# A three-block transformer kernel: recurrence scaling and gating order, row tails, attention buffers and decay weights rearranged

## Chip, cores, metric

The kernel runs on 1 core of one Trainium2 chip. The metric is the device time of one execution in microseconds (us); lower is better.

## What is computed

One input of 512 tokens x 1024 features, in float32, passes through three blocks. Each block is a mixer, a layer norm, a routed mixture of experts (MoE) and another layer norm. Cut to what matters here:

```python
# block 1: SSD (a chunked state-space scan, computed in this kernel as masked, decayed products) and
#          forgetting attention side by side, then w_out
y = y_diag + y_off + xs * d_skip                       # decay factors exp(a_cum_t - a_cum_s), causal
y = (y * silu(z)) * rsqrt(mean(square(y * silu(z))) + eps) * ssd_norm_g
probs = softmax(q k^T / 8 + F[t] - F[s])               # 8 heads of 64, causal
# block 2: differential attention, 8 heads, two softmaxes each
attn = p[:, :, 0] - lam * p[:, :, 1];  o = attn @ v;  o = o * rsqrt(mean(o*o) + eps) * subln_g * 0.8
# block 3: RWKV-7 time mix: token-shift mixes, low-rank w, a, g, and a recurrence per head
state = state * w_t + (state a_t) b_t + v_t k_t;  y_t = state r_t
y = groupnorm(y) * lnx_g + lnx_b + sum(r * k * r_k) * v;  out = (y * g) @ w_o
# each block: top-2 of 16, 32 and 32 experts (hidden size 512) per token, SwiGLU
```

## The kernel before

The program is a row of stages, each a block of five instruction streams (TensorE = PE, ScalarE = ACT, VectorE = DVE, GpSimd = POOL, SyncE = SP) that meet only at the stage's end. Within a stage the order on each engine is written out by hand and held together by semaphores; no scheduler reorders anything, so an instruction that waits holds all that stands behind it on its engine. Tokens lie in four tiles of 128 rows (j = 0 to 3). Weights of 2 MB a chunk go through a ring of six slots, which SP fills as the matmuls that used a slot finish; each expert has three such chunks. The stages, in order of time:

- `in_proj_stage` (block 1's projections), `ssd_and_attention_stage`, `project_and_experts(0)`.
- `norm_qkv_stage` (second norm of block 1, projections of block 2), `attention_stage`, `project_and_experts(1)`.
- `norm_rkv_stage` (second norm of block 2, projections of block 3), `wkv_stage` (the recurrence), `wkv_out_stage`, `project_and_experts(2)`, `last_norm_stage`.

**Decay weights** (L423 to L441, L738 to L858). For each of 8 heads a 128 x 1280 triangle of weights exp(min(0, decay)) is made. ACT writes the three off-diagonal pieces by Exp (`fade_off_diagonal`, L433). DVE writes the four diagonal 128 x 128 pieces as min(0, decay) (`clamp_diagonal`, L440). ACT takes Exp of these 512 columns (L781). DVE multiplies all 1280 columns with cb (L847), and PE multiplies per pair of heads (L744). Heads 0 to 2 are prepared in the stage before. Heads share four buffers, so heads 4 to 7 wait at L778 and L815 until the pair that used their buffer is through PE. Then `take_y` (L821, L822) adds the skip and gates, ACT squares (L763), PE sums (`sums`, L694, L695), and ACT turns the sums into inverse roots by Ln (L788) and Exp (L791), all ahead of its attention loop.

**Forgetting attention** (same stage, 16 steps) has three pairs of probability buffers. Each step: PE scores (L707, L710), DVE maxima (L827 to L829), ACT exponentials (L770), PE turns, ACT copies (L802), PE products, DVE copies out (L855). `norm_group` (L839) stands at steps 2 and 3 on DVE.

**Differential attention** (`attention_stage`, 32 steps) has the same loop with two pairs of buffers `prob`. In step s, PE does scores(s) (L922, L924), turn(s-2) (L938) and product(s-3) (L956). DVE does maxima(s) (L1020, L1021) and divide(s-1) (L1028, L1031, L1032), which combines the two softmaxes in place. turn(n) waits for divide(n).

**Row tails** (`norm_qkv_stage`, `norm_rkv_stage`). POOL gathers the experts' rows (L230). DVE adds them and takes statistics tile by tile (L244 to L252), ACT normalizes (L258, L260), PE turns the tile (`turn_rows`, L273), ACT takes it (`take_rows`, L281), and PE projects (L1601; L1772 for v). Before that PE runs 17 matmuls on constants (`keep_busy`, L265), of 128 x 512 in float32; each has two records in the trace. In `norm_rkv_stage` SP first loads eleven parameters on one semaphore. PE waits for the first nine, transposes `param_rows` (L1747), and only then turns rows; ACT waits for that transpose (L1786) before it normalizes tile 0. DVE mixes each tile with the tokens before (L1722 to L1712) for PE's v products.

**Recurrence** (`wkv_stage`). Eight turns, one for each pair of heads. In a turn PE doubles a triangular inverse in four rounds, each with two halves: squares (L2074), products (L2082), additions on DVE (`add_products`, L2346, which counts `d_tt` up by 8 a turn). The solves follow (`four`, L2090), each half copied out (L2272 by ACT, L2387 by DVE), then a serial chain of states (L2171, L2413). Between the first solves DVE prepares the next turn's operands (L2316, L2317). POOL finishes the rows of turn i-2:

```python
def finish_rows(n):
    pool.wait_ge(E["y_rstd"], n + 1)
    pool.wait_ge(d_tt, (n + 3) * 2 * ROUNDS)
    scaled_rows(pool, link, n, y_vars[n % 2])
    link(pool.tensor_tensor(rT[:, n, :], rT[:, n, :], y_added, ALU.add))
```

With n = i-2 this waits for all four rounds of turn i. The three operations are L1845, L1846, L1977, each over 128 x 512.

**After the recurrence** (`wkv_out_stage`). PE makes gate matmuls for eight column blocks (L1832, L1834; those of blocks 0 to 2, `EARLY_GATES`, come in the stage before) and transposes rows (L2493). ACT copies (L2504). DVE finishes the last pair's rows (L2509 to L2519) and only then multiplies gates in (L2523), block by block. PE's block c >= 4 waits for the multiplication of block c-4, whose PSUM bank it uses again.

## Time and profile before

| | us |
|---|---|
| time, median of 3 runs | 2727.61 (2724.8 to 2733.51) |
| profiled execution, its own time | 2733.16 |
| its span in the trace | 2731.4 |
| PE busy in it | 2366.0 (87%) |
| DVE, ACT, POOL busy | 1011.0, 564.9, 195.1 |
| granted TensorE clock, mean | 0.949 of full |

The profile is one execution, which took 5.6 us more than the median; its span leaves 1.8 us of its time outside. Times in its rows count from the start of the span. "Idle before" names who released a waiting engine. PEclk is the granted clock of TensorE in a stretch: 1.00 is 2.4 GHz, 0.50 is 1.2 GHz, and what lies between is a mixture of the two over the stretch.

### The profile page before, as it was taken

How to read it: one execution, taken by the hardware profiler on the slowest of the kernel's cores; microseconds unless marked ns; L12 is line 12 of the kernel's file. 1: busy time of each engine (PE TensorE's matmuls, PEld its weight loads, DVE VectorE, ACT ScalarE, POOL GpSimd, SP SyncE). 2: the span in 40 equal slices, each digit the busy share in tenths (PEclk: the TensorE clock that was granted, in tenths of full speed). 3: DMA queues.
4: the chain of work that ended last, by engine and by line, in shares of the span. 5: the costliest groups of instructions: out<-in, count | busy, mean ns of one | idle time of the engine just before them, and what ended most of it. 6: DMA issues, size and time to landing. Idle time of an engine off the chain costs nothing. (4 is left out here: it accounts for less than half of the span.)

```text
span 2731.4 us, 88107 instructions
## 1 busy us (share of the span) xinstructions
PE 2366.0 (87%) x38584; PEld 1611.1 (59%) x38585; DVE 1011.0 (37%) x2710; ACT 564.9 (21%) x1211; POOL 195.1 (7%) x309
## 2 busy tenths in 40 slices
PE   8997999999999888999767789978888988788982
PEld 4445557777444655777545533458777456566761
DVE  1216353333400854333212254046765353232324
ACT  2134211111300631111000031034332111011111
POOL 1002200000100010000000010012332100000001
PEclk9998999999999999999989889989999899899996
DMA  8211158976421006969999932000001269999995
GB/s 343 111 56 62 48 205 345 408 313 270 160 93 62 32 18 242 410 273 427 429 430 427 402 141 100 0 24 3 3 5 47 97 264 428 427 429 427 414 428 222
DMA packets 83423, 616.42 MB, mean 226 GB/s; under 512 B 19909, under 2 KB 40649, under 8 KB 49242
## 3 DMA queue, kind: packets, MB, share of 16 engines
q1 hardware_dynamic: 45664, 574.98, 50.9%
q10 hardware_dynamic: 31402, 20.06, 2.4%
q0 software_dynamic: 6224, 19.43, 2.2%
q8 instruction: 105, 1.72, 0.3%
q14 instruction: 28, 0.23, 0.0%
HBM read 582.92 MB, written 31.49 MB: 225 GB/s over the span
## 5 line engine op out<-in xcount | busy, mean ns | idle before, releaser
L1281 PE MATMUL ps<-ring,arena 128*32 128x128 f32 x13184 | 408.4, 283 | 104.7 <-DMA ring<-in_experts 71.9
L1281 PEld LDWEIGHTS ps<-ring,arena 128*32 128x32 f32 x13184 | 379.3, 114 | 146.3 <-DMA ring<-in_experts 69.8
L1258 PE MATMUL ps<-x_tok,arena 128*32 128x256 f32 x4768 | 291.3, 383 | 11.7 <-DVE arena L1396 8.3
L1489 DVE TENSOR_TENSOR arena<-arena,ps 128x64 f32<-128x64 f32 x292 | 64.8, 222 | 613.9 <-ACT arena L1341 613.9
L1341 ACT ACTIVATE arena<-ps 128x64 f32<-128x64 f32 x292 | 65.2, 223 | 1082.6 <-PE ps L1281 1082.6
L1281 PE MATMUL ps<-arena 128*32 128x128 f32 x5504 | 175.0, 287 | 45.5 <-DMA arena<-in_experts 37.0
L1258 PEld LDWEIGHTS ps<-x_tok,arena 128*32 128x32 f32 x4768 | 159.9, 111 | 89.4 <-issue 18.4
L1291 PE MATMUL ps<-ring,arena 128*32 128x256 f32 x3296 | 198.8, 380 | 12.4 <-DMA ring<-in_experts 12.2
L1281 PEld LDWEIGHTS ps<-arena 128*32 128x32 f32 x5504 | 160.8, 115 | 64.9 <-DMA arena<-in_experts 43.0
L1231 PE MATMUL ps<-ring,arena 128*128 128x512 f32 x384 | 172.3, 605 | 3.4 <-PEq L2460 1.7
L1291 PEld LDWEIGHTS ps<-ring,arena 128*32 128x32 f32 x3296 | 110.6, 110 | 83.6 <-DMA ring<-in_experts 20.3
L542 PE MATMUL ps<-xt_mem,ring 128*128 128x512 f32 x320 | 137.9, 593 | 0.0
L1231 PEld LDWEIGHTS ps<-ring,arena 128*128 128x128 f32 x384 | 73.1, 194 | 90.0 <-issue 89.7
L1476 DVE STREAM_TRANSPOSE arena<-ps 128x256 f32<-128x256 f32 x149 | 67.1, 450 | 148.7 <-PE ps L1258 148.7
L1775 PE MATMUL ps<-arena,ring 128*128 128x512 f32 x256 | 110.1, 593 | 0.0
L1601 PE MATMUL ps<-xt_mem,ring 128*128 128x512 f32 x256 | 110.0, 592 | 0.0
L542 PEld LDWEIGHTS ps<-xt_mem,ring 128*128 128x128 f32 x320 | 60.7, 190 | 76.4 <-issue 76.3
L1333 ACT ACT_TABLE_LOAD x73 | 93.7, 1283 | 33.0 <-DVE arena L1467 26.4
L1500 DVE COPY arena<-ps 128x256 f32<-128x256 f32 x146 | 62.0, 425 | 93.0 <-PE ps L1291 93.0
L1291 PE MATMUL ps<-xt_mem,arena 128*32 128x256 f32 x1376 | 83.4, 380 | 5.0 <-DMA xt_mem<-in_experts 3.9
L1775 PEld LDWEIGHTS ps<-arena,ring 128*128 128x128 f32 x256 | 48.6, 190 | 61.5 <-issue 61.5
L1601 PEld LDWEIGHTS ps<-xt_mem,ring 128*128 128x128 f32 x256 | 48.7, 190 | 61.1 <-issue 61.1
(437 smaller groups left out, 2990.0 us busy)
## 6 DMA issues: line engine op xcount, KB each, us to landing
ring<-in_experts SPq DMA_DIRECT2D x165, 2048.0 KB, 20.8
arena<-in_experts SPq DMA_DIRECT2D x50, 2048.0 KB, 24.9
xt_mem<-in_experts SPq DMA_DIRECT2D x25, 2048.0 KB, 29.7
ring<-in_mixer_chunks SPq DMA_DIRECT2D x24, 2048.0 KB, 12.6
xybuf<-arena ACTq DMA_DIRECT2D x608, 32.0 KB, 6.7
xybuf<-arena SPq DMA_DIRECT2D x1, 9216.0 KB, 51.2
ring<-gate_rows SPq DMA_DIRECT2D x2, 2048.0 KB, 7.1
rows<-in_ln_g POOLq DMA_DIRECT2D x6, 512.0 KB, 7.5
```

Source lines behind the costliest of these rows:

```text
L542: ins = pe.matmul(bank, w[:, k, j * P:(j + 1) * P], xT[:, k, :], start=(k == 0), stop=(k == NK - 1))
L1231: ins = pe.matmul(ps[:, 2 * j + c, :], mT[:, k, j * P:(j + 1) * P], w[:, k, :], start=(k == 0), stop=(k == NK - 1))
L1258: ins = pe.matmul(ps[to, 5, 0:W], one_hot[:, j, :], x_tok[:, j, q * W:(q + 1) * W], start=(j == 0), stop=(j == NT - 1))
L1281: ins = pe.matmul(ps[at, 2 + half, 0:P], xg[:, k, :], w_gu[half][:, k, q, :], start=(k == 0), stop=(k == NK - 1))
L1291: ins = pe.matmul(ps[at, 4, 0:W], hT[:, f, :], w_d[:, f, q * W:(q + 1) * W], start=(f == 0), stop=(f == NT - 1))
L1333: act.preload_act_table(ACT.Silu)
L1341: act.activation(silu_g[:, half, :], ps[:, 2 + half, 0:HALF], ACT.Silu).then_inc(s_silu[half], 1)
L1476: dve.transpose(xg.rearrange("p k s -> p (k s)"), ps[:, 5, 0:W]).then_inc(s_xg, 1)
L1489: dve.tensor_tensor(hidden[:, half, :], silu_g[:, half, :], ps[:, 2 + half, HALF:P], ALU.mult)\
L1500: dve.tensor_copy(y_sb[:, b, :], ps[:, 4, 0:W]).then_inc(s_y, 1)
L1601: ins = pe.matmul(ps[:, n % 8, :], lhs, rhs, start=(k == 0), stop=(k == NK - 1))
L1775: ins = pe.matmul(bank, w[:, k, j * P:(j + 1) * P], xm[:, k, :], start=(k == 0), stop=(k == NK - 1))
```

## The change

Seven parts, each a rearrangement; the values computed stay the same. (1) All 8 heads' weights get buffers of their own, in ring slots 4 and 5, `xt_mem` and `rows`. The waits for buffers go. The clamp of heads 3 to 7 moves from DVE to ACT, as Relu of the negated difference followed by Exp with scale -1. The chunk that used slot 5 is loaded a stage later. (2) ACT's inverse roots move behind the first two steps' exponentials, into other PSUM banks; `norm_group` moves from steps 2 and 3 to 4 and 5. (3) Differential attention gets a third pair of buffers and turns and multiplies one step later. (4) `keep_busy` is 13 matmuls instead of 17 in both tails. (5) In `norm_rkv_stage` tile 0 is turned ahead of the parameter transpose, which waits for six loads; the three low-rank weights are loaded behind the arrival of tile 0's rows, on a semaphore of their own. (6) In the recurrence POOL waits for three rounds of turn i, not four. (7) In `wkv_out_stage` DVE multiplies the first three gates ahead of finishing the last rows.

```diff
-        head_weights = [view(slot(4), n * TRI, TRI) for n in range(3)] + [view(xt_mem, 2 * TRI, TRI)]
+        head_weights = [view(slot(4 + h // 3), h % 3 * TRI, TRI) for h in range(6)] + [view(xt_mem, 2 * TRI, TRI), view(rows, 0, TRI)]
         def weights(h):
-            return head_weights[2 * (h // 2 % 2) + h % 2]
+            return head_weights[h]
+        def fade_head(act, h):
+            fade_off_diagonal(act, h)
+            for i in range(NT):
+                at = slice(i * P, (i + 1) * P)
+                ins = act.activation(weights(h)[:, at], decay_rows[:, h, at], ACT.Relu, bias=gate_c_tok[:, i, h:h + 1], scale=-1.0)
+            return ins
...
-                    stream_mixer(sp, first + 11, first + 12)
...
-                    stream_mixer(sp, c + 2, c + 3)
+                    stream_mixer(sp, c + 2, c + 4)
...
-                        if h >= 4:
-                            act.wait_ge(pe_c.sem, y0 + h // 2 - 1)
-                        fade_off_diagonal(act, h)
-                        act.wait_ge(dve_b.sem, c0 + h + 1)
-                        act.activation(weights(h)[:, 0:T], weights(h)[:, 0:T], ACT.Exp).then_inc(act_a.sem, 1)
+                        fade_head(act, h).then_inc(dve_b.sem, 1)
+                        act.wait_ge(dve_b.sem, c0 + h - EARLY_HEADS + 1)
+                        act.activation(weights(h)[:, 0:T], weights(h)[:, 0:T], ACT.Exp, scale=-1.0).then_inc(act_a.sem, 1)
...
                     for s in range(jobs + 3):
+                        if s == 2:
+                            inverse_roots()
                         if s < jobs:
                             exps(s)
...
-                        if s in (2, 3):
-                            norm_group(s - 2)
+                        if s in (4, 5):
+                            norm_group(s - 4)
...
-            prob = [[view(xt_mem, (2 * b + c) * T, T) for c in range(2)] for b in range(2)]
+            prob = [[view(xt_mem, (2 * b + c) * T, T) for c in range(2)] for b in range(2)] + [[view(rows, c * T, T) for c in range(2)]]
...
-                        if 0 <= s - 2 < jobs:
-                            turn(s - 2)
+                        if 0 <= s - 3 < jobs:
+                            turn(s - 3)
...
-                        if 0 <= s - 3 < jobs:
-                            product(s - 3)
+                        if 0 <= s - 4 < jobs:
+                            product(s - 4)
...
-                    keep_busy(pe, 17)
+                    keep_busy(pe, 13)
...
+                    sp.wait_ge(rows_in[0].sem, n0["rows"][0] + 32)
+                    for dst, src in ((lora_w, a["rw_w1_2"][0]), (lora_a, a["rw_a1_2"][0]), (lora_g, a["rw_g1_2"][0])):
+                        sp.dma_start(dst, src.rearrange("(k p) n -> p k n", p=P)).then_inc(lora_in.sem, 16)
...
-                    keep_busy(pe, 17)
-                    pe.wait_ge(mixer_params.sem, p0 + 16 * 9)
-                    pe.transpose(ps[:, 7, 0:P], param_rows, ident).then_inc(tr.sem, 1)
+                    keep_busy(pe, 13)
                     turn_rows(pe, 0, n0)
+                    pe.wait_ge(mixer_params.sem, p0 + 16 * 6)
+                    pe.transpose(ps[:, 7, 0:P], param_rows, ident).then_inc(param_turned.sem, 1)
...
                         norm_rows(act, j, n0)
                         take_rows(act, j, n0)
+                        if j == 0:
+                            act.wait_ge(param_turned.sem, t0 + 1)
...
-                        pool.wait_ge(d_tt, (n + 3) * 2 * ROUNDS)
+                        pool.wait_ge(d_tt, (n + 2) * 2 * ROUNDS + 6)
...
+                    for c in range(EARLY_GATES):
+                        gate(c)
                     scaled_rows(dve, link, LAST, y_vars[LAST % 2])
...
-                    for c in range(NK):
+                    for c in range(EARLY_GATES, NK):
+                        gate(c)
```

## Rows read from the trace of the kernel before

**Rows 1.** Block 2's experts: us, PE, PEld, DVE, ACT, POOL busy, PEclk, DMA share, GB/s
```profile
1080.00:1570.00 490.00, 394.10 (x9867) 303.45 (x9857) 133.84 (x466) 55.29 (x130) 0.01 (x1) 0.93 0.95 400
```
**Rows 2.** Timeline of the decay weights (start, us, engine, line, idle before)
```profile
202.34 1.31 ACT L433 ACTIVATE xt_mem<-ring,small 128x384 f32<-128x384 f32 x3 [1.22 <-PEq L468]
...
212.99 0.87 DVE L440 TENSOR_SCALAR ring<-ring,small 128x128 f32<-128x128 f32 x4
...
221.45 1.49 DVE L847 TENSOR_TENSOR xt_mem<-xt_mem 128x1280 f32<-128x1280 f32 x1
```
**Rows 3.** ACT's groups by form in the decay weights (busy, mean ns)
```profile
L781 ACT ACTIVATE ring<-ring 128x512 f32<-128x512 f32 x3 | 1.9, 620 | 1.5 <-DVE ring L440 1.5
...
L433 ACT ACTIVATE ring<-ring,small 128x128 f32<-128x128 f32 x3 | 1.2, 387 | 0.0
```
**Rows 4.** ACT's timeline where forgetting attention starts
```profile
233.61 1.28 ACT L791 ACT_TABLE_LOAD   x1
...
235.96 0.35 ACT L770 ACTIVATE xt_mem<-ps,small 128x128 f32<-128x128 f32 x1
...
241.88 0.58 ACT L770 ACTIVATE rows<-ps,small 128x384 f32<-128x384 f32 x1 [4.22 <-DVE small L829]
```
**Rows 5.** DVE's timeline there
```profile
230.67 0.17 DVE L829 TENSOR_SCALAR small<-small 128x2 f32<-128x2 f32 x1
...
239.68 0.97 DVE L827 TENSOR_TENSOR ps<-ps,ring 128x768 f32<-128x768 f32 x1 [2.73 <-PE ps L710]
```
**Rows 6.** Waits in four heads of differential attention, 910.7 to 951.7 (total, times, longest)
```profile
PE ps L938 <- DVE xt_mem L1032: 6.6, 5, 1.3
DVE small L1020 <- PE ps L924: 2.7, 8, 0.4
```
**Rows 7.** Timeline of the tail before block 2's projections
```profile
697.76 17.91 PE L265 MATMUL ps<-cst 128*128 128x512 f32 x34 [4.16 <-PEq L1145]
...
710.64 1.24 ACT L260 ACTIVATE x_tok<-x_tok,small 128x1024 f32<-128x1024 f32 x1 [0.48 <-DVE small L252]
...
715.50 1.04 PE L273 MATMUL ps<-cst,x_tok 128*128 128x128 f32 x8
```
**Rows 8.** Timeline of the tail before block 3's projections
```profile
1570.03 16.98 PE L265 MATMUL ps<-cst 128*128 128x512 f32 x34 [8.01 <-PEq L1145]
...
1582.70 0.21 DVE L249 BATCH_NORM_AGGREGATE small<-small 128x2 f32<-128x12 f32 x1
...
1588.99 0.33 PE L1747 MATMUL ps<-cst,ring 128*128 128x128 f32 x1 [1.98 <-DMA ring<-in_rw_g]
...
1591.61 1.97 PE L273 MATMUL ps<-cst,x_tok 128*128 128x128 f32 x8 [2.30 <-ACT x_tok L260]
```
**Rows 9.** Busy time by turn of the recurrence, from one L2316 to the next
```profile
1876.87:1912.20 35.33, 31.25 (x874) 28.92 (x870) 25.09 (x56) 14.93 (x26) 11.23 (x17) 1.00 0.01 4
1912.20:1948.80 36.60, 31.51 (x874) 29.04 (x870) 26.28 (x56) 14.93 (x26) 12.45 (x18) 1.00 0.01 3
...
1985.20:2023.07 37.87, 32.73 (x874) 30.39 (x870) 26.27 (x55) 14.93 (x26) 12.44 (x18) 0.95 0.01 3
```
**Rows 10.** Timeline of one turn, DVE, POOL and PE
```profile
2017.83 0.75 DVE L2346 TENSOR_TENSOR ring<-ring,ps 128x256 f32<-128x256 f32 x2
...
2020.57 1.04 POOL L1845 TENSOR_TENSOR arena<-arena,small 128x512 f32<-128x512 f32 x1 [10.74 <-DVE ring L2346]
...
2023.04 1.26 POOL L1977 TENSOR_TENSOR arena<-arena,ring 128x512 f32<-128x512 f32 x1
...
2023.07 1.77 DVE L2316 SCALAR_TENSOR_TENSOR xt_mem<-ring 128x512 f32<-128x512 f32 x1
...
2026.23 1.09 PE L2090 MATMUL ps<-ring 64*64 64x128 f32 x16 [1.05 <-DVE ring L2387]
```
**Rows 11.** Timeline after the recurrence
```profile
2121.30 2.07 PE L1832 MATMUL ps<-rows,arena 128*128 128x512 f32 x2 [2.66 <-DVE arena L2523]
```
**Rows 12.** Busy time by stretch after the recurrence
```profile
2122.00:2132.00 10.00, 10.00 (x18) 3.49 (x16) 1.89 (x4) 1.19 (x2) 1.12 (x1) 0.50 0.79 303
```

More of the change, by code:

```diff
@@ L647, in ssd_and_attention_stage @@
             logs = [zT[:, 2 * g, :] for g in range(GROUPS)]
-            c0, e0, p0 = dve_b.take(HEADS), act_a.take(HEADS), ln_done.take(HEADS)
+            c0, e0, p0 = dve_b.take(HEADS - EARLY_HEADS), act_a.take(HEADS), ln_done.take(HEADS)
             y0, z0, q0 = pe_c.take(PAIRS), scaled.take(PAIRS), ev.take(PAIRS)
@@ L693, in sums @@
                         pe.wait_ge(ev.sem, q0 + 2 * g + 2)
-                        pe.matmul(ps[:, 4 + g, :], ones, zT[:, 2 * g, :], start=True, stop=False)
-                        pe.matmul(ps[:, 4 + g, :], ones, zT[:, 2 * g + 1, :], start=False, stop=True).then_inc(mm.sem, 1)
+                        pe.matmul(ps[:, 7 - g, :], ones, zT[:, 2 * g, :], start=True, stop=False)
+                        pe.matmul(ps[:, 7 - g, :], ones, zT[:, 2 * g + 1, :], start=False, stop=True).then_inc(mm.sem, 1)
                     def scores(n):
@@ L785, in _, with inverse_roots @@
                         square(p)
-                    for g in range(GROUPS):
-                        act.wait_ge(mm.sem, s0 + g + 1)
-                        act.activation(logs[g], ps[:, 4 + g, :], ACT.Ln, bias=eps_ln, scale=1.0 / 256).then_inc(sq.sem, 1)
-                    act.wait_ge(sq.sem, r0 + GROUPS)
-                    for g in range(GROUPS):
-                        act.activation(logs[g], logs[g], ACT.Exp, scale=-0.5).then_inc(sq.sem, 1)
+                    def inverse_roots():
+                        for g in range(GROUPS):
+                            act.wait_ge(mm.sem, s0 + g + 1)
+                            act.activation(logs[g], ps[:, 7 - g, :], ACT.Ln, bias=eps_ln, scale=1.0 / 256).then_inc(sq.sem, 1)
+                        act.wait_ge(sq.sem, r0 + GROUPS)
+                        for g in range(GROUPS):
+                            act.activation(logs[g], logs[g], ACT.Exp, scale=-0.5).then_inc(sq.sem, 1)
                     for s in range(jobs + 3):
+                        if s == 2:
+                            inverse_roots()
                         if s < jobs:
@@ L888, in attention_stage @@
             for s in range(STEPS):
-                if 0 <= s - 2 < jobs:
-                    order["tile", s - 2] = len(order)
+                if 0 <= s - 3 < jobs:
+                    order["tile", s - 3] = len(order)
                 if s in turned_at:
@@ L991, in _ @@
                                 act.wait_ge(dve_a.sem, x0 + n_comp * s + c + 1)
-                                if s >= 2:
-                                    act.wait_ge(tr.sem, t0 + order["tile", s - 2] + 1)
-                                act.activation(prob[s % 2][c][:, 0:width(s)], score(s, c), ACT.Exp,
+                                if s >= 3:
+                                    act.wait_ge(tr.sem, t0 + order["tile", s - 3] + 1)
+                                act.activation(prob[s % 3][c][:, 0:width(s)], score(s, c), ACT.Exp,
                                                bias=st[:, s % DEEP, 2 + c:3 + c], scale=SCALE,
                                                accum_out=st[:, s % DEEP, 4 + c:5 + c]).then_inc(act_a.sem, 1)
-                        n = s - 2
+                        n = s - 3
                         if 0 <= n < jobs:
@@ L1029, in divide @@
                         if n_comp == 2:
-                            p0, p1 = (p[:, 0:width(n)] for p in prob[n % 2])
+                            p0, p1 = (p[:, 0:width(n)] for p in prob[n % 3])
                             link(dve.tensor_scalar(m[:, 7:8], m[:, 7:8], m[:, 4:5], lam, ALU.mult, ALU.mult))
@@ L1664, in norm_rkv_stage @@
             done = {"v": 8, "w": 9, "a": 10, "g2": 12, "r": 20}
-            t0, n0, l0, d0 = tr.take(1), tail_bases(), loaded.total, dve_b.take(1)
-            m0, e0, p0 = mm.take(28), ev.take(28), mixer_params.take(16 * 11)
+            param_turned, lora_in = pe_c, rows_spread
+            t0, n0, l0, d0 = param_turned.take(1), tail_bases(), loaded.total, dve_b.take(1)
+            m0, e0, p0, r0 = mm.take(28), ev.take(28), mixer_params.take(16 * 8), lora_in.take(16 * 3)
             x0, c0 = dve_a.take(NT + 5), consts.take(3)
@@ L1793, in _ @@
                         take_rows(act, j, n0)
+                        if j == 0:
+                            act.wait_ge(param_turned.sem, t0 + 1)
+                            act.activation(mu, ps[:, 7, 0:6 * NK].rearrange("p (n k) -> p n k", n=6), ACT.Copy)
+                            act.activation(par, ps[:, 7, 6 * NK:(6 + N_PAR) * NK].rearrange("p (n k) -> p n k", n=N_PAR), ACT.Copy)\
+                               .then_inc(consts.sem, 1)
                     for n, job in enumerate(jobs):
@@ L2516, in _, with gate @@
                     dve.wait_ge(dve_a.sem, x0 + 3)
+                    def gate(c):
+                        dve.wait_ge(ev.sem, e0 + c + 1)
+                        dve.wait_ge(mm.sem, m0 + c + 1)
+                        dve.tensor_tensor(mT[:, c, :], mT[:, c, :], ps[:, c % 4, :], ALU.mult).then_inc(dve_b.sem, 1)
+                    for c in range(EARLY_GATES):
+                        gate(c)
                     scaled_rows(dve, link, LAST, y_vars[LAST % 2])
```

42 lines of the change are left out of this document (14 added, 28 removed).

## The prediction

> **What bounds the kernel now.** I read the busy times by stretch first, then the timelines of the stages that the diff touches, then the waits. PE is busy for 87% of the span, but three kinds of stretch differ. In projections PE is the bound. In block 2's experts DMA moves 400 GB/s at a share of 0.95 [rows 1], so PE's speed decides little there; what counts is when that stage starts. Attention, tails and recurrence are chains in which engines take turns, and there a wait costs what it lasts. All seven parts lie in such chains.
>
> **Do early gains reach the end?** SP loads an expert chunk only when PE has used the one before (L1164), and the third expert's after the logits (L1149). So the stream begins with PE's work in its own stage, and a stage that starts earlier ends earlier. I count every gain in full, and make its loss a rival.
>
> **Part 1, weights.** Before, head 7's product starts at 221.45 on DVE, and the last pair's matmuls follow it [rows 2]. After, ACT makes heads 3 to 7 without a wait for a buffer, starting at 202.34. Per head: three Exp pieces 1.31, as now; four Relu of 128 columns; Exp of 512 columns 0.62. No Relu runs in the trace. Its nearest row is the Exp piece of 128 columns at 0.387 [rows 3]; pieces overlap (three pieces show 1.31 in one merged row), so four cost between 3 x 0.387 = 1.16 and 4 x 0.387 = 1.55. I take 1.2, as the overlap is seen. A head is then 3.1, five heads are 15.5, and one square of 512 columns (0.62 like the Exp) stands among them: 202.34 + 16.1 = 218.4. DVE's product starts 3.0 sooner. DVE has no clamp left (five times 0.87 [rows 2]) and its products of 1.49 fit between. **Gain 3.0**, at 1.55 a head 1.3, at 1.16 3.2. The chunk moved a stage later is a 2 MB load in a stage with a quiet DMA, used by the second expert over 150 us later: 0.
>
> The Trainium skill ("ScalarE: Activation LUTs", rules for kernel authors) says to put relu on VectorE, not ScalarE. By that rule the move is wrong: 1.2 on ACT for 0.87 on DVE, 1.6 lost over five heads if ACT alone counts. The rows bear out the price but not the verdict, since what goes with the move are the waits for buffers and the ping-pong of two engines.
>
> **Part 2, inverse roots.** Before, maxima(0) are ready at 230.84 [rows 5], but ACT's first exponential starts at 235.96, behind a table load and two Exps [rows 4]. PE's scores(2) need that exponential; DVE idles 2.73 for them and starts at 239.68 [rows 5]; ACT's exps(2) start at 241.88 after 4.22 idle [rows 4]. After, exps(0) and exps(1) run at 231 to 233.7. The roots follow: two loads of 1.28, two Ln and two Exp of about 0.6 each, 5.0 in all, to 238.7. Meanwhile PE makes scores(2) and (3) and DVE their maxima. exps(2) then start at 238.7, 3.2 sooner. Step 3, bound by DVE, comes about 4.2 sooner. `norm_group` in steps 4 and 5 falls where DVE idles. **Gain 4.1**, bounds 2.5 (a wait for the roots' banks comes back) and 5.1 (the whole 5.1 between 230.84 and 235.96).
>
> **Part 3, third pair.** In four heads PE idles 6.6 on divide (L1032) and DVE idles 2.7 on scores (L924) [rows 6]. The late turn delays the next scores, which delay DVE. With one step more between them the turn finds its input ready. PE's idle time goes first; then DVE is the bound, and only its own idle time can be won: 2.7 / 4 = 0.67 a head, 5.4 for eight, less the first head's filling. **Gain 4.7**, bounds 0 and 5.4. The added step is empty at the end; its price there is order, not work: 0 to 0.5, inside these bounds.
>
> **Part 4, `keep_busy` before block 2's projections.** 34 records take 17.91, to 715.5, and the turn of tile 0 stands behind them, though ACT had the tile ready at 710.64 + 1.24 = 711.9 [rows 7]. The eight records that go run at full clock at 0.43 apart, 3.4 in all (by the mean, 17.91 x 8 / 34 = 4.2, but the slow ones stand in front). PE is free at 712.1, just behind the tile. **Gain 3.4**, bounds 2.5 and 3.6 (the tile's own time). PE's work after it is unbroken, so all of it counts.
>
> **Part 5, tail before block 3.** Statistics of tile 0 are done at 1582.9. In rows 7 the normalization starts 1.1 after the same point and takes 1.24, so the tile would be ready at 1585.0. Before, PE idles for the last of the low-rank weights until 1588.99, ACT waits for the transpose, and the turn starts at 1591.61 [rows 8]. Without them the turn starts at 1585.0, 6.6 sooner; 26 records end at 1583.6. On the other side ACT's two parameter copies (0.3) now stand behind tile 0. The three loads (1.15 MB) no longer share DMA with tile 0's rows: 0 to 0.9. SP's wait for these rows holds only loads needed after v. **Gain 6.9**, bounds 5.5 and 8.5.
>
> **Part 6, recurrence.** POOL starts its three operations at 2020.57, when the fourth round is in, and ends at 2024.30. DVE's L2316 starts at 2023.07 and takes 1.77 [rows 10]. It reads two SBUF operands, as POOL does, and ends 0.54 after POOL: it waited. The copy behind it is late, and PE idles 1.05. Turns show the price: 35.33 in a turn in which POOL has nothing to finish, 36.60 in one in which it has, 37.87 with the clock at 0.95 [rows 9]. After, POOL starts at 2018.7, behind the third round (2018.58), and ends at 2022.5, 0.6 before L2316. In its new place DVE runs L2312, L2346 and a copy, each with PSUM as one operand. Five turns (2 to 6) have both. At 1.0 to 1.3 each that is 5.0 to 6.4; three of them also lost 1.3 by clock (37.87 less 36.60), up to 3.9 more. **Gain 7.3**, bounds 4 and 9.5.
>
> The Trainium skill ("SBUF — State Buffer", who interferes with whom) has the same picture as an exclusive lock: a VectorE instruction with two SBUF inputs blocks on a running GpSimd instruction. The trace agrees, 1.77 beside POOL. By that rule POOL's new place is free of it.
>
> **Part 7, first gates.** PE idles 2.66 for the first gate multiplication [rows 11], which stands behind three operations of DVE. After, it is ready before PE asks. The last rows are finished some 2.1 later (three multiplications of 512 columns, at 0.7 each: 1.49 x 512 / 1280 = 0.6 and a start); block 7, which needs them, comes three blocks of 4.8 after block 4. A block is 2.07 for L1832, another 2.07 for L1834 with as many columns, and four transposes at half of the 1.97 that eight took at a low clock [rows 8], 5.1 less overlap. **Gain 2.7.** In 2122 to 2132 PE is fully busy at granted clock 0.50, 1.2 GHz [rows 12]; what it did just before was to idle these 2.66. Without that the clock may hold: four blocks are 19 and would halve, 9.6, of which I allow 7.3, since ACT and DVE have to keep up. What idled less may lower the clock later all the same, so I add only 1.3. Bounds 2.0 and 10.
>
> **Sum.** 3.0 + 4.1 + 4.7 + 3.4 + 6.9 + 7.3 + 4.0 = 33.4. The profiled execution goes from 2733.2 to 2699.8. The median before lies 5.6 lower, so it becomes 2727.6 - 33.4 = 2694.2.
>
> **Rivals.**
> - *A. The buffers give nothing and the clock stays low.* DVE idles only 0.67 a head on scores [rows 6], so there is little to win if its own operations bound the loop; the dips in the recurrence may come from elsewhere. Gain 3.0 + 4.1 + 0 + 3.4 + 6 + 5 + 2.2 = 23.7: 2703.9. Chance 0.22.
> - *B. The clock holds after the recurrence.* PE would be busy without a gap; against it, the clock was low at 2122 to 2132 with PE fully busy. Gain 33.4 + 6 to 8: 2687. Chance 0.10.
> - *C. The DMA stream swallows what lies ahead of it* (the change doesn't arrive). For it speaks a share of 0.95 [rows 1]; against it, that the loads wait for PE. Then only a few us of the total move: 2725. Chance 0.04.
> - *D. Slower: the tails start cold.* `keep_busy` holds the clock until the tile comes. If PE, freed 3.4 sooner, idles and the clock falls to 1.2 GHz in either tail, block 3's turn shows the price of that: 1.97 for 1.04. Half speed loses as much time as the work takes at full clock. To end slower by 8.2 it has to eat the 33.4 and 8.2 more, so it decides from 42 us of PE work at 1.2 GHz on; over 96 us in the two projection stages together it gives 2694 + 96 = 2790. Against it, PE ends at 712.1 with the tile at 711.9. Chance 0.02.
>
> **How the numbers follow.** The likeliest case, all parts in place, has 0.62: 2694, with its own range 2687 to 2702. About 0.3%, 8.2 us, is what a measurement can tell from no change. Least gains summed make 18 (2710), the largest 45 (2682), but not all err one way. The range 2684 to 2707 takes in A and B. Faster by over 0.3%: 0.94; within: 0.04; slower: 0.02.
>
> **What would show it.** Right: no PE wait on L1032 and DVE nearly without gaps in differential attention; L2316 far below 1.77 in all turns, turns of 35.5; the turn of tile 0 some 14.4 after the tail's start in block 2, 15 in block 3; no PE wait ahead of block 4's gates. Wrong: a table load beside each Relu (1.28 each), L2346 longer than 0.75 a pair [rows 10], new PE waits in the turns of the third pair, or an experts' stage that grew by what was won ahead of it.

## The result, and the profile after

The changed kernel takes 2697.98 us (median of four runs, 2697.32 to 2698.91) against 2726.97 for the kernel before (2724.8 to 2733.51): 29.0 us less. The two medians by themselves give 0.9894; the ratio on record is 0.9881, 95% interval 0.9865 to 0.9896, which holds both. Run again in a later session it took 2697.02 (2695.11 to 2698.77) against 2727.39, 30.4 less, ratio 0.9889 (0.9870 to 0.9909). The forecast was 2694, a ratio of 0.9878. The kernel before scatters more than the changed one: 2720.8 to 2737.5 over all its runs, with medians of 2726.97, 2731.2, 2727.39 and 2733.11 in four sessions. So a difference of two medians is good to some 3 us only.

The stages tell more than the totals. The table gives their lengths in two profiled executions of each kernel, read from the starts and ends of the first and last matmuls of each stage. "Before" is the profile above and a second one of the same kernel (`c0_before_again` below), "after" the changed kernel's and its repetition (`a1_after_again`).

| stage, parts of the change | before | after | gain | forecast |
|---|---|---|---|---|
| decay weights to forgetting attention's end, 1 and 2 | 101.1, 101.0 | 94.4, 94.4 | 6.6 | 7.1 |
| experts of block 1 | 310.5, 309.4 | 310.8, 310.4 | -0.6 | 0 |
| last expert matmul to turn of tile 0, block 2's tail, 4 | 21.9, 21.9 | 18.2, 18.4 | 3.6 | 3.4 |
| block 2's projections | 171.3, 171.3 | 171.3, 171.3 | 0 | 0 |
| differential attention, 3 | 101.8, 101.7 | 98.6, 99.0 | 3.0 | 4.7 |
| experts of block 2 | 488.1, 487.7 | 490.1, 490.1 | -2.2 | 0 |
| last expert matmul to turn of tile 0, block 3's tail, 4 and 5 | 29.6, 28.6 | 21.1, 21.7 | 7.7 | 6.9 |
| v products, other projections of block 3 | 205.4, 204.1 | 204.9, 204.5 | 0 | 0 |
| recurrence, 6 | 315.0, 314.1 | 308.8, 308.3 | 6.0 | 7.3 |
| row transposes after it, 7 | 26.3, 26.3 | 15.6, 15.7 | 10.6 | 4.0 |
| experts of block 3 | 462.9, 462.9 | 464.5, 464.2 | -1.4 | 0 |

The rows add up to 33.3, and the stages that aren't in the table differ by under 1 us; the spans, 2731.4 and 2725.6 before, 2695.6 and 2695.0 after, differ by 33.2 in the mean. The forecast's 33.4 was met by a sum in which one term came out much larger, two smaller, and the experts took 3.6 to 4.2 back.

The two profiles of a kernel agree to 1.2 us in each row, but the same code in the other runs of this document spreads wider. From the decay weights to forgetting attention's end the code of before takes 101.0 to 103.7 (three profiles) and that of after 93.1 to 94.7 (eight); the recurrence 314.1 to 316.6 and 306.9 to 308.8; the experts of block 1 take 309.2 to 311.0 in all kernels. The gains of the parts stand clear of this, the differences of 1 to 2 us do not.

**Decay weights and roots.** Timeline of the changed kernel, ACT and DVE:

```profile
203.71 1.26 ACT L436 ACTIVATE ring<-ring,small 128x128 f32<-128x128 f32 x4
...
218.30 1.49 DVE L848 TENSOR_TENSOR rows<-rows,xt_mem 128x1280 f32<-128x1280 f32 x1 [1.53 <-ACT rows L790]
...
230.47 1.28 ACT L798 ACT_TABLE_LOAD   x1
...
235.39 0.56 ACT L781 ACTIVATE rows<-ps,small 128x384 f32<-128x384 f32 x1
```

Four Relu take 1.26 in a row (1.2 was taken), and head 7's product starts at 218.30 where 218.4 was worked out and 221.45 stood before [rows 2]. The roots stand behind the first four exponentials; step 2's first exponential starts at 235.39 (before 241.88 [rows 4]; the working has 238.7, which leaves part 1's 3.0 out, so 235.7 with both). Attention itself, from its first score to its last product, takes 69.9 where it took 73.1.

**Differential attention.** Waits in four heads of the changed kernel, 899.8 to 938.7:

```profile
PE ps L957 <- ACT arena L976: 2.7, 4, 0.7
...
DVE small L1021 <- PE ps L925: 1.3, 4, 0.3
```

PE's wait for the divide, 6.6 us before [rows 6], is gone. A head takes 9.86 us where it took 10.25. DVE still waits for scores, 1.3 where it was 2.7, and PE has a new wait, 0.67 a head: `product` now waits for ACT's `store_tile`.

**Tails.** Timeline of the changed kernel, tail of block 2 and of block 3:

```profile
691.48 14.22 PE L265 MATMUL ps<-cst 128*128 128x512 f32 x26 [4.16 <-PEq L1146]
...
704.05 1.24 ACT L260 ACTIVATE x_tok<-x_tok,small 128x1024 f32<-128x1024 f32 x1 [0.48 <-DVE small L252]
...
705.53 1.04 PE L273 MATMUL ps<-cst,x_tok 128*128 128x128 f32 x8
...
1557.83 12.84 PE L265 MATMUL ps<-cst 128*128 128x512 f32 x26 [7.17 <-PEq L1146]
...
1569.08 0.21 DVE L249 BATCH_NORM_AGGREGATE small<-small 128x2 f32<-128x12 f32 x1
...
1571.75 1.09 PE L273 MATMUL ps<-cst,x_tok 128*128 128x128 f32 x8 [1.09 <-ACT x_tok L260]
```

The turn starts 14.1 and 13.9 after the tail's start; 14.4 and 15 were forecast. In block 3 PE waits 1.09 for the normalized tile and for nothing else.

**Recurrence.** Busy time by turn, columns as in [rows 9], and the timeline of a turn:

```profile
1820.76:1856.09 35.33, 31.23 (x874) 28.97 (x870) 25.02 (x55) 14.75 (x25) 6.62 (x12) 1.00 0.01 3
1856.09:1891.80 35.71, 31.25 (x874) 28.91 (x870) 25.19 (x56) 14.95 (x26) 12.47 (x17) 1.00 0.01 3
...
1927.48:1964.25 36.77, 31.46 (x874) 29.00 (x870) 25.10 (x56) 14.94 (x26) 12.48 (x17) 1.00 0.01 3
```
```profile
1935.72 0.28 PE L2168 MATMUL ps<-ring 64*64 64x64 f32 x2 [1.21 <-issue]
...
1959.92 1.04 POOL L1850 TENSOR_TENSOR arena<-arena,small 128x512 f32<-128x512 f32 x1 [8.90 <-DVE ring L2351]
...
1962.39 1.27 POOL L1982 TENSOR_TENSOR arena<-arena,ring 128x512 f32<-128x512 f32 x1
...
1964.25 0.68 DVE L2321 SCALAR_TENSOR_TENSOR xt_mem<-ring 128x512 f32<-128x512 f32 x1
```

POOL ends at 1963.66, 0.59 before DVE's L2321, which takes 0.68 in place of 1.77 [rows 10], in all turns. No stretch of low clock is left in the turns. But the later turns take 36.2 to 36.8 and not 35.5: PE has an idle stretch without a visible cause ("issue") of 1.21, 0.69 and 0.64 us in three of them.

**After the recurrence.** Busy time of the whole stretch of row transposes, the kernel before and after (us, then PE, PEld, DVE, ACT, POOL busy, PEclk, DMA share, GB/s):

```profile
2113.00:2139.60 26.60, 23.61 (x52) 9.59 (x52) 10.85 (x15) 5.08 (x10) 9.72 (x7) 0.62 0.62 237
```
```profile
2086.60:2102.50 15.90, 15.53 (x52) 7.53 (x52) 11.22 (x15) 5.12 (x10) 9.30 (x7) 0.90 0.66 233
```

The same 52 matmul records take 23.61 us at a granted clock of 0.62 before, 15.53 at 0.90 after. The idle time accounts for 2.7 of the 10.6, the clock for the other 8.

### The profile page after: what moved, and what is told of

Read it like the earlier page. It is cut to its first block and busy times, and to the rows that moved or that the text cites. A ratio compares the mean times of both kernels' runs of the same rounds, so it can differ in the third digit from the quotient of the medians.

```text
span 2695.6 us, 88071 instructions
## 1 busy us (share of the span) xinstructions
PE 2343.1 (87%) x38568; PEld 1597.3 (59%) x38569; DVE 1000.8 (37%) x2690; ACT 571.8 (21%) x1231; POOL 194.1 (7%) x309
## 5 line engine op out<-in xcount | busy, mean ns | idle before, releaser
L1334 ACT ACT_TABLE_LOAD x73 | 93.7, 1283 | 33.1 <-DVE arena L1468 26.4
L1501 DVE COPY arena<-ps 128x256 f32<-128x256 f32 x146 | 62.0, 425 | 94.7 <-PE ps L1292 94.7
```

The lines of the kernel that those rows point to most:

```text
L1334: act.preload_act_table(ACT.Silu)
L1501: dve.tensor_copy(y_sb[:, b, :], ps[:, 4, 0:W]).then_inc(s_y, 1)
```

## The experiments

**The kernel before, again** (no edit).

> The kernel before, unchanged, profiled a second time. The profile of before took 2733.2 us, 6 above its median. Theory: one stage is longer in that execution by chance (most likely a low-clock stretch, as after the recurrence), and this profile shows a span of about 2725 with that stage shorter. Rival: the spread sits in the DMA-bound experts' stages, some 2 us in each of three. In either case the stages in which engines take turns repeat to within 0.3 us.

It took 2727.3, span 2725.6. Stages of turns repeat (101.0, 21.9, 101.7, 26.3 us), and the low clock after the recurrence is there again, so it is not chance. The 5.8 us of difference lie in the start (1.1), the experts (1.5) and block 3's tail with the v products (2.2), and 0.9 in the recurrence: mostly the rival's places, in no single one.

**Part 7 undone.**

```diff
-                    for c in range(EARLY_GATES):
-                        gate(c)
...
-                    for c in range(EARLY_GATES, NK):
+                    for c in range(NK):
```

> The changed kernel with part 7 undone alone. Between the first row transpose and the last one after the recurrence the changed kernel takes 15.6 us where before took 26.3. Theory (the idle 2.66 us of PE brings on the low clock): the gap of 2.7 returns, the clock falls to 0.50 behind it, and the stretch takes 25 to 27, total +9 to +11, 2707 to 2709. Rival (the clock's fall there belonged to the dips in the recurrence, which part 6 removed): only the gap returns, +2.7, 2700.7, and the stretch takes 18 to 19.

2704.69 (2700.12 to 2709.17), ratio 0.9915 (0.9892 to 0.9938); the stretch takes 26.4. Windows and timeline of this kernel:

```profile
2083.00:2109.50 26.50, 21.62 (x50) 8.34 (x48) 10.36 (x15) 5.23 (x10) 9.24 (x7) 0.68 0.63 238
```
```profile
2090.80 2.08 PE L1837 MATMUL ps<-rows,arena 128*128 128x512 f32 x2 [4.29 <-DVE arena L2526]
```

PE idles 4.29 for the first gate product, and the matmul behind it runs at half speed (2.08 for two records that take 1.02 at full clock). The turns of the recurrence ahead of it had no stretch of low clock. The theory holds for the stretch, 10.8 longer. The total rose by 6.7 (against 2697.98) or 7.7 (2697.02) and not by 9 to 11: in the profiled execution the recurrence and block 2's experts are 1.7 and 2.1 shorter than the mean of after's two.

**Part 7 alone**, on the kernel before (the new `gate` and its two loops, as in the diff of the change).

> The kernel before with part 7 alone. Theory (the idle time sets the clock): the gap of 2.66 goes, the clock holds at 1.00 from the second block on, and the stretch from first to last row transpose falls from 26.3 to 16 to 18: total 9 to 11 less, 2716 to 2718. Rival (the clock falls anyway, because the recurrence ahead of it has dips): only 2.7 less, 2724. The prediction's own value for this part lies between, 4.0 less.

2722.20 (12 runs, 2713.0 to 2725.0) beside 2731.2 for the kernel before in the same session: ratio 0.9967 (0.9953 to 0.9982). Windows and timeline:

```profile
2114.40:2129.80 15.40, 14.24 (x52) 6.18 (x52) 11.24 (x15) 4.98 (x10) 9.31 (x7) 1.00 0.65 230
```
```profile
2119.20 1.12 PE L1832 MATMUL ps<-rows,arena 128*128 128x512 f32 x2 [0.82 <-DVE arena L2520]
```

The stretch falls by 11.2, to 15.1, with the clock at 1.00 throughout, although four dips lay in the recurrence ahead. Both directions of this part give the same: at this place 2.66 us of idle PE bring the clock to 1.2 GHz for the work behind, 0.82 do not.

This profile shows something else. Its first attention stage is the code of before, and it takes 103.7 where before's two profiles take 101.1 and 101.0; from the first score to the last product 77.3 for 73.1. So one profile of that stage can be off by 2.6 (it bears on part 2 below).

**Part 6 undone.**

```diff
-                        pool.wait_ge(d_tt, (n + 2) * 2 * ROUNDS + 6)
+                        pool.wait_ge(d_tt, (n + 3) * 2 * ROUNDS)
```

> The changed kernel with part 6 undone alone. Theory: five turns get 1.05 back as PE's wait on the copy behind the first operand preparation, which takes 1.77 again, and with it the short stretches of low clock of turns 4 to 6; recurrence +5 to +9, total 2703 to 2707. Rival (the low-clock stretches were chance or come from what lies ahead of the stage): only +5.3, 2703, with the clock at 1.00 in turns 4 to 6. A third: the PE gaps without a visible cause of 1.21, 0.69 and 0.64 us in turns 4 to 6 of the changed kernel are caused by the earlier POOL work; then they vanish here and the return is 2.8 only.

Recurrence 314.6, 6.0 longer than the mean of after's two. Windows by turn and one turn's timeline:

```profile
1889.20:1925.60 36.40, 31.25 (x872) 28.90 (x870) 26.19 (x55) 14.94 (x26) 12.46 (x17) 1.00 0.01 3
1925.60:1963.40 37.80, 31.48 (x872) 29.00 (x870) 26.19 (x55) 14.95 (x26) 12.46 (x17) 1.00 0.01 3
```
```profile
1963.40 1.27 POOL L1982 TENSOR_TENSOR arena<-arena,ring 128x512 f32<-128x512 f32 x1
1963.43 1.78 DVE L2321 SCALAR_TENSOR_TENSOR xt_mem<-ring 128x512 f32<-128x512 f32 x1
...
1966.60 1.09 PE L2095 MATMUL ps<-ring 64*64 64x128 f32 x16 [1.06 <-DVE ring L2392]
```

DVE's 1.78 and PE's 1.06 are back, 5.3 in five turns, but the clock stays at 1.00 in the turns shown; of the three dips of the kernel before one is there, in the last turn. So the rival is right for this run: the wait doesn't bring all dips back. But it goes with them. The four profiles with POOL's late wait have 3, 3, 4 and 1 dips in the turns (`before`, `c0_before_again`, `p7_gates_only`, this one), the ten without it none. The "issue" gaps are still there (1.17 and 0.53), so POOL's new place doesn't make them either. The total is 2698.17 (2696.70 to 2700.50): in its profiled execution the first attention stage took 93.1 and the small projection stage behind the transposes 83.8, where the changed kernel took 94.4 and 85.4. The total can't show this part; the stage does.

**The changed kernel, again** (no edit).

> The changed kernel, unchanged, again, as the measure for the three beside it and for the part that undid POOL's scaling. Theory: every stage but the first attention stage, the experts and the recurrence repeats to 0.1 us; the stretch of row transposes after the recurrence takes 15 to 16 us, the recurrence 307 to 309; total 2694 to 2699. Rival: the short stretch after the recurrence was luck of one execution, and here it takes 20 or more.

Mostly as expected: 2697.02, recurrence 308.3, transposes 15.7. But some stages differ by more than the 0.1 expected: block 3's tail by 0.6, differential attention by 0.5, the projections of block 3 by 0.4. The two profiles' experts differ by 0.3 at most.

**Part 3 undone** (two pairs; turn, product and store each one step earlier).

```diff
-            prob = [[...] for b in range(2)] + [[view(rows, c * T, T) for c in range(2)]]
+            prob = [[...] for b in range(2)]
...
-                        if 0 <= s - 3 < jobs:
-                            turn(s - 3)
+                        if 0 <= s - 2 < jobs:
+                            turn(s - 2)
```

> The changed kernel with part 3 undone alone: two pairs of buffers in differential attention. The third pair saved 4.1 us up to the last score (86.9 to 82.8) and gave back 0.9 at the stage's end. Theory: the stage is 3.2 longer, all of it in PE's waits for the divide (L1033), total +3.2. Rival (the shorter attention was the clock's, two low stretches of 3.4 us less in it): +1.5 or less with the divide waits back.

The stage takes 101.4, 2.6 more than after's mean, and the waits return, here in 904 to 945:

```profile
PE ps L939 <- DVE xt_mem L1033: 5.3, 4, 1.3
DVE small L1021 <- PE ps L925: 2.7, 8, 0.4
```

The period is 10.25 again, for 9.86. The mechanism is shown. The total, 2697.51 (2694.77 to 2700.28) beside 2697.02, doesn't show it: the small projection stage behind the row transposes took 83.8 for 85.4, and the 3.4 us of low clock that stand at its start in the changed kernel are missing.

**Clamps back on DVE, eight buffers kept.**

```diff
-                        fade_head(act, h).then_inc(dve_b.sem, 1)
+                        fade_off_diagonal(act, h)
...
+                    clamp_diagonal(dve, EARLY_HEADS).then_inc(dve_b.sem, 1)
                     for h in range(HEADS):
+                        if h + EARLY_HEADS + 1 < HEADS:
+                            clamp_diagonal(dve, h + EARLY_HEADS + 1).then_inc(dve_b.sem, 1)
```

> The changed kernel with the clamps of heads 3 to 7 back on DVE, one head's four pieces of 0.87 ahead of each product; the eight buffers stay. Theory (both engines are loaded evenly after the change, so the move matters and not the buffers alone): DVE then has five clamps of 0.87, eight products of 1.49 and three take_y of about 1.4 ahead of the last product's end, 20.4 us in a row from 202.4, where ACT's chain gave 218.4 plus 1.5: forgetting attention starts 2.5 to 3 us later. Rival (the Trainium skill, ScalarE: Activation LUTs, relu belongs on VectorE, and the buffers alone made the gain): it starts 1 to 1.6 us earlier, as ACT is freed of 1.2 us a head.

2691.69 (2691.03 to 2693.87) beside 2697.02 (2695.11 to 2698.77) in the same session, ratio to the kernel before 0.9869 (0.9850 to 0.9888). My theory of 2.5 to 3 us more failed. Timeline and windows of this kernel, and the same window of the changed one:

```profile
219.26 1.48 DVE L851 TENSOR_TENSOR rows<-rows,xt_mem 128x1280 f32<-128x1280 f32 x1
```
```profile
219.00:224.00 5.00, 3.21 (x30) 2.13 (x31) 3.84 (x5) 0.63 (x1) 0.00 (x0) 1.00 0.92 354
```
```profile
219.00:224.00 5.00, 4.16 (x29) 2.73 (x30) 2.46 (x4) 0.63 (x1) 0.00 (x0) 0.66 0.96 331
```

The last product starts 0.9 later, counted from the last projection (18.35 for 17.47), but the last pair's matmuls (30 and 29 records in these windows) then run at full clock, 3.21 us for 4.16, and attention starts 0.5 earlier (24.0 for 24.5). To the end of forgetting attention the stage takes 92.5, 1.9 less than after (94.4).

Neither gain can be put down to the edit. `m6_scales_late` runs the changed kernel's own code in this stage, with Relu on ACT, and in it the last pair met full clock too. Its last product, the window that starts as far ahead of it, and its first score:

```profile
216.99 1.49 DVE L848 TENSOR_TENSOR rows<-rows,xt_mem 128x1280 f32<-128x1280 f32 x1 [1.38 <-ACT rows L790]
216.75:221.75 5.00, 3.22 (x30) 2.13 (x31) 3.59 (x4) 1.35 (x3) 0.00 (x0) 1.00 0.78 256
222.67 0.61 PE L714 MATMUL ps<-cst 128*128 128x128 f32 x4
```

From the last projection (199.52) attention starts 23.2 behind, 0.9 ahead of this run: with the last pair at full clock in both, Relu on ACT is worth the 0.9 of the product. The other 1.4 of the 1.9 lie in attention itself, 68.5 for 69.9, and 68.5 is also what it takes in `k1_fill_gaps`, `m5_params_first` and `d9_busy_9`, whose code there is the changed kernel's. The Trainium skill ("ScalarE: Activation LUTs", rules for kernel authors) says relu on VectorE. This run doesn't bear that out for this place: ACT's 1.26 for DVE's 0.87 costs more by itself, but the product starts 0.9 sooner with it. Of the 3.3 us that the product gained over the kernel before (20.77 to 17.47), the buffers gave 2.4 and the Relu 0.9. In the two profiled executions another 1.0 lies in block 1's experts (309.4 for 310.4), which the edit doesn't touch; why the medians differ by 5.3 stays open.

**Filling PE's gaps at the recurrence's start**: `keep_busy(pe, 5)` ahead of its first matmuls and again ahead of the first `low`.

> The changed kernel with five constant matmuls of 128x512 ahead of the recurrence's first matmuls and five more ahead of its first triangle products, where PE idles 4.6 and 4.8 us and the granted clock then is 0.50 for 20 us. Theory (idle PE time brings on the low clock, as after the recurrence): the clock stays at 1.00 there, and 9.6 us of matmuls at half speed shrink by up to 4.8, of which chains on DVE hide a part: 2 to 4 us less. Rival (these stretches are bound by DVE, ACT and POOL): clock 1.00, but at most 0.5 us less. A third: the filling overruns the gaps and costs up to 1 us.

2694.02 (2692.90 to 2698.64). Windows of this kernel and of the changed one, from the recurrence's start on:

```profile
1778.50:1806.50 28.00, 20.73 (x235) 13.25 (x234) 16.36 (x32) 9.23 (x13) 8.34 (x24) 0.88 0.18 57
```
```profile
1776.60:1804.60 28.00, 13.81 (x211) 12.17 (x211) 16.38 (x32) 8.81 (x13) 8.38 (x24) 0.63 0.17 57
```

The clock rises from 0.63 to 0.88, and the recurrence takes 308.6, as after (308.8, 308.3). The second filling took 6.25 us in a gap of 4.8. The rivals hold: in this stretch, where PE waits for other engines in turn, the low clock costs little, and the filling its overrun.

**Part 5's order undone**: parameters transposed ahead of tile 0, weights loaded at once, but on their own semaphore.

```diff
-                    sp.wait_ge(rows_in[0].sem, n0["rows"][0] + 32)
...
-                    turn_rows(pe, 0, n0)
                     pe.wait_ge(mixer_params.sem, p0 + 16 * 6)
                     pe.transpose(ps[:, 7, 0:P], param_rows, ident).then_inc(param_turned.sem, 1)
+                    turn_rows(pe, 0, n0)
```

> The changed kernel with the order of part 5 undone: parameters are transposed ahead of tile 0 again, and the low-rank weights are loaded without waiting for tile 0's rows, but on the semaphore of their own, so PE's transpose waits for six small loads only. From the tail's start to the turn of tile 0 the changed kernel takes 13.9 to 14.4 us, before took 21.6. Theory (what cost 7 us was the wait for the low-rank weights, not the order): the turn starts within 0.5 of the changed kernel's, ACT's two copies add 0.3, so 14 to 15; total +0 to +1. Rival (the order carries the gain, since even the six loads land late or the weights share DMA with the rows): 17 to 21, total +3 to +7.

2695.11 (2694.72 to 2696.61), span 2693.4. Timeline:

```profile
1557.20 14.46 PE L265 MATMUL ps<-cst 128*128 128x512 f32 x26 [7.36 <-PEq L1146]
...
1571.51 0.27 PE L1748 MATMUL ps<-cst,ring 128*128 128x128 f32 x1
...
1571.78 1.09 PE L273 MATMUL ps<-cst,x_tok 128*128 128x128 f32 x8
```

The parameters' transpose runs without any wait behind `keep_busy`, and tile 0 follows 14.6 after the tail's start, within 0.2 of the changed kernel's repetition. The order is worth nothing; the separate semaphore, with `keep_busy` at 13, is worth 7 us. Not all of that is the semaphore's: 17 constant matmuls took 16.98 here [rows 8], so with them tile 0 could not have turned before 17.0. By that estimate some 3 us of the tail's 7.7 need part 4 as well.

**Part 2 undone**: `inverse_roots()` at s == 0, `norm_group` at steps 2 and 3 (banks as after).

> The changed kernel with the inverse roots back ahead of ACT's attention loop and the group norms back at steps 2 and 3. Part 2 gave 3.2 us in forgetting attention (73.1 to 69.9). Theory: ACT's first exponential waits 5 us behind two table loads, two Ln and two Exp again and DVE's third maxima with it; the stage takes 72.5 to 73.5, total +3. Rival (the third buffer pair and two fewer stretches of low clock made the 3.2): 70 to 71, total under +1.

Attention takes 75.5, and the whole stage 101.4, 7.0 more than after and as much as before (101.1). Waits in 230 to 242 and ACT's timeline:

```profile
PE ps L714 <- ACT xt_mem L781: 3.9, 1, 3.9
```
```profile
238.31 0.58 ACT L781 ACTIVATE rows<-ps,small 128x384 f32<-128x384 f32 x1 [3.56 <-DVE small L833]
```

The profiled execution, 2704.64, is the longest of four (median 2696.69, from 2693.3). In it part 1's head start of 3.3 us at the last product doesn't reach the stage's end. Whether that is the rule one profile can't tell: with the roots in front attention takes 73.1, 73.1, 77.3 and 75.5 in four profiles, of which the first three are one code, and their stretches of low clock fall in different places. With the roots behind it takes 68.5 to 70.0 in ten. So part 2 is worth 3.1 us or more in every pair of these profiles; its usual size, and whether parts 1 and 2 add up, stays open. The total doesn't show it: the other three executions took 2693.3 to 2697.1, no more than the changed kernel.

**`keep_busy` at 9.**

> The changed kernel with keep_busy at 9 matmuls instead of 13 in both tails. PE then idles 3.4 to 4.5 us ahead of the first turned tile. The case of the prediction in which the tails start cold: the turn of tile 0 starts at the same time as with 13 (14.1 and 13.9 us after the tail's start), but the clock falls to 0.50 in it and behind it, the eight transposes take 1.97 instead of 1.04, and what PE does next (171.3 us of projections in block 2, v's 68 in block 3) grows by 1 to 10 us a stage. Rival (only the time before the tile counts): nothing changes beyond 0.3 us in either stage.

2697.83 (2697.55 to 2698.11). Timeline and windows of block 2's tail, and the changed kernel's window of the same length:

```profile
703.17 1.97 PE L273 MATMUL ps<-cst,x_tok 128*128 128x128 f32 x8 [4.29 <-ACT x_tok L260]
```
```profile
703.00:717.00 14.00, 11.70 (x24) 5.75 (x25) 7.26 (x12) 4.43 (x11) 0.00 (x0) 0.64 0.45 189
```
```profile
705.50:719.50 14.00, 11.44 (x39) 5.91 (x38) 6.97 (x11) 7.09 (x19) 0.00 (x0) 1.00 0.43 177
```

The turn stands 0.2 to 0.3 earlier, the eight transposes take 1.97 in place of 1.04, and block 2's projections take 174.7 for 171.3, block 3's v products 68.6 for 68.2 and 67.8. That is the mechanism of the prediction's rival D, at 4 us, not 42. But 13 matmuls aren't safe either: in three of ten profiles with 13 (`k1_fill_gaps`, `m2_roots_first`, `m5_params_first`) block 2's projections took 174.2, 174.4 and 172.8, while the three profiles with 17 all have 171.3. Differential attention behind them took 99.8 in three of these four runs, where it takes 98.5 to 99.0 in the others with three pairs of buffers. So where this comes it costs 1.6 to 4.6 us in all; part 4 gains 3.6 there. Whether 17 prevents it or three are too few was not tried.

**Clamps split**, a version meant to be better: DVE clamps heads 3 and 4 behind its first two products, ACT takes 5 to 7.

```diff
+                        if h < 5:
+                            fade_off_diagonal(act, h)
+                        else:
+                            fade_head(act, h).then_inc(dve_b.sem, 1)
...
+                        if h == 2:
+                            for n in (3, 4):
+                                clamp_diagonal(dve, n).then_inc(dve_b.sem, 1)
```

> A version meant to beat the changed kernel: DVE clamps heads 3 and 4, behind its first two products; ACT takes heads 5 to 7 by Relu; the eight buffers stay. ACT's chain ends at about 217 (three heads at 3.1, two at 1.9, one square), DVE's products and clamps at about 218 to 219, where the changed kernel ended the last product at 219.7 and the version with all clamps on DVE at 220.7. Theory: forgetting attention starts at 224 to 224.5, 1 to 1.5 us earlier, total 2695 or a little less. Rival (the last pair's matmuls at low clock end the stretch, not the products): it starts at 225.2 to 225.7 as in both others.

2692.14 (2690.43 to 2695.01), ratio 0.9858 (0.9841 to 0.9874). Timeline and windows:

```profile
218.09 1.49 DVE L854 TENSOR_TENSOR rows<-rows,xt_mem 128x1280 f32<-128x1280 f32 x1 [1.45 <-ACT rows L793]
```
```profile
219.00:224.00 5.00, 4.36 (x29) 2.92 (x30) 2.20 (x4) 0.63 (x1) 0.00 (x0) 0.66 1.03 351
```

The product is 0.3 earlier, still waits 1.45 for ACT, and the clock is 0.66 behind it: attention starts at 225.4, as in the changed kernel and as the rival said. The span of 2688.7 has its gain elsewhere (the projection stage 83.8, block 3's tail, recurrence 307.1), in places that the edit doesn't touch. Both versions of the clamp lie 5 us below the changed kernel's medians (this one in a session in which that kernel wasn't run); for neither is the difference traced to the edit.

## Why the prediction was right, and where it was not

- **The sum** was right: 33.4 forecast, 33.2 between the spans, 29.0 and 30.4 between the medians, a ratio of 0.9878 for 0.9881 and 0.9889. Every term has the sign that was forecast; that the sum came out so close is luck. Part 7 gave 6.6 more than forecast, part 5's tail 0.8 and part 4's 0.2; part 3 fell short by 1.7, part 6 by 1.3, parts 1 and 2 by 0.5, and the experts, put at nothing, took 4.2.
- **Part 7** is the term that was mis-sized: "I add only 1.3" for the clock. The row read right ("the clock may hold: four blocks are 19 and would halve") gave 9.6, and 8 came. I discounted it for no row's sake; part 7 undone and alone show 10.8 and 11.2. 10.6 lies outside the bounds of 2.0 to 10. That was rival B, given 0.10, in mechanism and price; the total is not B's, since other terms fell short.
- **Part 3** gave 3.0 for 4.7. The step that failed is "PE's idle time goes first; then DVE is the bound, and only its own idle time can be won: 0.67 a head". A new wait took its place, PE's L957 for ACT's `store_tile`, 0.67 a head, and 0.39 a head were won. At the end the added step took 0.9 back, above the bound of 0.5. Rival A's "the buffers give nothing" is refuted by the run with two.
- **Parts 1 and 2** gave 6.6 for 7.1: attention starts 3.4 sooner (3.0 forecast) and is 3.2 shorter (4.1). Head 7's product stands 0.1 from where the working put it. By the runs 0.9 of part 1 is the Relu on ACT, the rest its buffers. The term of part 2 is 3.1 or more in every pair of profiles; why it gave 3.2 and not 4.1 between before and after is not known.
- **Part 4** gave 3.6 for 3.4, but in three of ten profiles the projections and the attention behind it cost 1.6 to 4.4, as much as the part gains or more. **Part 5** gave 7.7 for 6.9 by the mechanism "PE idles for the last of the low-rank weights". The order, counted in the same term, is worth nothing. Its 1585.0 is 1585.2 by its own terms (1582.9 + 1.1 + 1.24).
- **Part 6** gave 6.0 for 7.3. The wait is as predicted (1.77 to 0.68, PE's 1.05 gone five times, 5.3). The step "three of them also lost 1.3 by clock" was mis-sized: the dips are gone in all profiles with POOL early, but with part 6 undone only one of three comes back, and "issue" gaps of 2.5 in all came in their place.
- **Do early gains reach the end?** "I count every gain in full" held for all but 3.6 to 4.2 us. In block 2's experts the loss arises in the first 45 us. Windows of the changed kernel, the whole stage (it answers to [rows 1]) and two stretches of these 45 us:

```profile
1060.50:1550.60 490.10, 398.74 (x10016) 309.06 (x10016) 136.45 (x482) 56.67 (x130) 0.00 (x0) 0.94 0.96 401
...
1080.60:1090.60 10.00, 8.35 (x207) 6.66 (x200) 3.15 (x11) 0.45 (x2) 0.00 (x0) 1.00 1.02 428
1090.60:1100.60 10.00, 8.52 (x190) 7.07 (x187) 2.08 (x8) 1.73 (x3) 0.00 (x0) 0.83 1.01 429
```

DMA moves what it moved before. A stretch of low clock of 3.4 us lies in the second. One batch of 128 matmuls in it, in the changed kernel and in `m7_gates_late`, which has no such stretch:

```profile
1092.69 5.37 PE L1282 MATMUL ps<-ring,arena 128*32 128x128 f32 x128 [1.48 <-issue]
1093.12 3.70 PE L1282 MATMUL ps<-ring,arena 128*32 128x128 f32 x128 [1.48 <-issue]
```

The batch takes 1.67 longer behind the same idle time. Nine of the eleven profiles of changed versions have one in these 45 us, and the stage then takes 489.7 to 490.8; the two without take 487.9 and 489.1, the three profiles of before and of part 7 alone, also without, 487.7 to 488.6. So what speaks from the profiles is not the DMA stream swallowing gains (rival C) but PE's clock in a stage that I had called insensitive to it: "PE's speed decides little there". No run set this stretch by itself, 0.5 of the 2.2 is not in that batch, and why the stretch comes there after the change stays open. The loss of 1.4 in block 3's experts was not traced; the changed versions take 462.7 to 464.6 there.

## What to carry to other kernels

An idle stretch of PE ahead of dense matmuls can cost itself and then the clock, as after the recurrence: price it with the matmuls behind it at half speed, and don't discount that without a row. Where engines take turns, the same low clock costs little in one place and much in another: taking 14 of 20 us of it away at the recurrence's start gained nothing, but in the turns a dip of 3.4 us cost 1.3 [rows 9]. Give loads that the first work doesn't need a semaphore of their own before reordering anything. When single parts are worth less than the scatter of totals, compare stages, and in more than two profiles: two agreed to 1.2 us, but the same code in other runs was up to 2.7 off. Before a gain is put down to an edit, see whether a run without the edit has it too.

## What the runs showed that was not expected

- Idle PE time of 2.66 and 4.29 us ahead of the gate blocks brought the clock from 2.4 to 1.2 GHz for the work behind; 0.82 us did not. The stretch took 26.3 and 26.4 against 15.1 to 15.7.
- PE has gaps without a visible cause in the recurrence's later turns after the change (1.21, 0.69, 0.64 us), also with part 6 undone (1.17, 0.53), none in two profiles of the kernel before and one of 0.55, in an earlier turn, with part 7 alone. Their cause was not found.
- In projection stages of equal code the length takes few values: 171.3, or 172.8 to 174.7; 85.3 to 85.5, or 83.8. They go with where stretches of low clock fall. So do block 1's experts: 310.4 to 311.0 in the eight profiles with 3.4 us of low clock at their start, 309.2 to 309.4 in the six without.
